# Forgetting attention: q and k of four heads in one 512-column accumulator, from two half-depth chunks

## The reference

```python
proj = x @ w_in                                    # (512, 1024) @ (1024, 4 * 1024 + 16)
q, k, v, g, f_logit = jnp.split(proj, [D, 2 * D, 3 * D, 4 * D], axis=-1)
qh, kh = _rms_norm(heads(q), qn_g), _rms_norm(heads(k), kn_g)      # 16 heads of 64
c = jnp.cumsum(jax.nn.log_sigmoid(f_logit + b_f), axis=1)
s = einsum('bhqd,bhkd->bhqk', qh, kh) * 64 ** -0.5 + (c[..., :, None] - c[..., None, :])
o = einsum('bhqk,bhkd->bhqd', softmax(where(causal, s, -1e30)), v)
h = (o * sigmoid(g)) @ w_out
```

## Time and profile before

| | us |
|---|---|
| median of 3 runs (lowest, highest) | 1371.62 (1370.80, 1373.13) |
| the profiled execution, its own time | 1372.18 |
| its span, first to last instruction | 1370.40 |
| TensorE busy | 1338.7 (98%) |
| GpSimd, ScalarE, DVE busy | 528.1, 493.6, 472.9 |
| mean granted TensorE clock | 0.995 |

### The profile page before, as it was taken

One profiled execution on the slowest core, in us unless ns is written; L12 is line 12 of the kernel. 1 busy time (PEld: TensorE's weight loads), 2 busy tenths in 40 slices (PEclk: granted clock), 3 DMA queues, 4 the chain that ended last, 5 costly groups with the idle time before them and its releaser, 6 DMA issues.

```text
span 1370.4 us, 18953 instructions
## 1 busy us (share of the span) xinstructions
PE 1338.7 (98%) x7304; PEld 1118.0 (82%) x7304; DVE 472.9 (35%) x936; ACT 493.6 (36%) x823; POOL 528.1 (39%) x421
## 2 busy tenths in 40 slices
PE   7999999799999999999999999999999999999997
PEld 6888877689888888888888888777898888888886
DVE  4364447682111111011644565544641111110105
ACT  3413266533223322211366565644232233222111
POOL 4422441215444444643234222323145444445440
PEclk9999999999999999999999999999999999999999
DMA  6301131203333332333124212212233333323321
GB/s 210 121 32 62 63 122 62 62 17 107 96 109 103 93 93 77 124 107 95 62 63 126 63 32 63 63 62 75 80 93 95 108 105 94 93 83 118 104 96 61
DMA packets 141416, 119.60 MB, mean 87 GB/s; under 512 B 5680, under 2 KB 120592, under 8 KB 141328
## 3 DMA queue, kind: packets, MB, share of 16 engines
q1 hardware_dynamic: 141088, 118.10, 27.6%
q10 hardware_dynamic: 240, 0.31, 0.1%
HBM read 116.20 MB, written 2.10 MB: 86 GB/s over the span
## 4 chain that ended last, share of the span: by engine, by line
PE 92%; DVE 4%; ACT 3%; issue 1%; DMA 0%; ACTq 0%; SPq 0%; DVEq 0%
PE banks L531 27%; PE banks L532 27%; PE banks L533 27%; PE banks L915 2%; PE banks L1073 1%; PE banks L1038 1%; PE banks L611 1%; PE banks L1054 1%; ACT w_hi L1231 1%; PE banks L933 1%; PE banks L988 1%; PE banks L975 1%; PE banks L1046 0%; DMA x_res<-in_x_dram 0%; PE banks L1024 0%
## 5 line engine op out<-in xcount | busy, mean ns | idle before, releaser
L1184 POOL TENSOR_TENSOR w_lo<-w_raw,w_hi 128x512 fp32r<-128x512 f32 x417 | 527.8, 1293 | 810.9 <-ACT w_hi L1231 657.9
L531 PE MATMUL banks<-xT_lo,w_hi 128*128 128x512 f32 (+2 forms) x1024 | 385.0, 376 | 1.3 <-DVEq L1581 1.0
L533 PE MATMUL banks<-xT_hi,w_hi 128*128 128x512 f32 (+2 forms) x1024 | 380.9, 372 | 0.0
L532 PE MATMUL banks<-xT_hi,w_lo 128*128 128x512 f32 (+2 forms) x1024 | 380.8, 372 | 0.0
L1231 ACT ACTIVATE w_hi<-w_raw 128x2048 fp32r<-128x2048 f32 (+2 forms) x106 | 198.1, 1869 | 173.4 <-PE banks L533 145.0
L531 PEld LDWEIGHTS banks<-xT_lo,w_hi 128*128 128x128 f32 (+1 forms) x1024 | 192.4, 188 | 36.3 <-issue 3.8
L533 PEld LDWEIGHTS banks<-xT_hi,w_hi 128*128 128x128 f32 (+1 forms) x1024 | 192.3, 188 | 34.0
L532 PEld LDWEIGHTS banks<-xT_hi,w_lo 128*128 128x128 f32 (+1 forms) x1024 | 192.5, 188 | 32.2
L1850 DVE TENSOR_TENSOR banks<-silu_g,banks 128x512 f32<-128x512 f32 x44 | 30.6, 696 | 402.5 <-PE banks L533 402.5
L531 PE MATMUL banks<-w_lo,xT_hi 128*128 128x256 f32 (+1 forms) x480 | 158.6, 330 | 2.5 <-issue 2.4
L533 PE MATMUL banks<-w_hi,xT_hi 128*128 128x256 f32 (+1 forms) x480 | 153.3, 319 | 0.0
(11 more groups left out here) (193 smaller groups left out, 1244.1 us busy)
## 6 DMA issues: line engine op xcount, KB each, us to landing
w_raw<-in_ffn_w_dram SPq DMA_DIRECT2D x92, 512.0 KB, 4.5
w_raw<-in_ffn_w_dram SPq DMA_DIRECT2D x20, 1024.0 KB, 4.8
w_raw<-in_fox_w_in_dram SPq DMA_DIRECT2D x16, 1024.0 KB, 5.8
w_raw<-in_even_w_in_dram SPq DMA_DIRECT2D x13, 1024.0 KB, 4.9
w_raw<-in_even_w_out_dram SPq DMA_DIRECT2D x4, 1024.0 KB, 4.8
w_raw<-in_fox_w_out_dram SPq DMA_DIRECT2D x4, 1024.0 KB, 4.8
x_res<-in_x_dram SPq DMA_DIRECT2D x4, 512.0 KB, 6.8
out_dram<-x_res SPq DMA_DIRECT2D x3, 512.0 KB, 2.6
```

The source lines that it names most:

```text
L531: mm(acc, l_hi, r_lo, start=first, stop=False)
L532: mm(acc, l_lo, r_hi, start=False, stop=False)
L533: return mm(acc, l_hi, r_hi, start=False, stop=final)
L1184: ins = nc.gpsimd.tensor_tensor(w_lo[c % RING][:, a:a + n], w_raw[c % RAW][:, a:a + n], w_hi[c % RING][:, a:a + n].bitcast(F32), ALU.subtract)
```

## The change

q and k of the same four heads come side by side in one accumulator of 512 columns. A head group (stage `foxh0` to `foxh3`) is two chunks, each of half the depth (4 of 8 row blocks) and 256 columns of q beside 256 of k, loaded by two DMAs of 512 KB. The number and size of chunks stay. A piece is now one token tile of one half: 4 x 3 = 12 matmuls of 512 columns, and a tile's accumulator is closed by its second half. Copy, square, sums, root and norm are done once for 8 heads of a tile, and the turn is four transposes into bank 3, read by two copies (one for q, one for k, since their gains differ). `sq` has one buffer and `qn` two, where they had two and three. The order of pieces is written out (`HEAD_LEAD`, `HEAD_ORDER`), and so is the list of roundings with what holds their quarters back (`fox_rounds`). `fox_start(0)` now runs four pieces, the first half and the second half of tiles 0 and 1, each first piece waiting for its own tile. The second half chunk `foxh0` is rounded in the norm before, ahead of the fourth tile's root. The quarters of both `foxh0` chunks and of the first `foxv0` chunk are waited for one by one. The copy to `c_rows` stands before the load of the second chunk of `foxh1`.

```diff
-FOX_LEAD = [("q", 0), ("k", 0), ("v", 0)]
-FOX_PARTS = [[("q", 1), ("k", 1), ("v", 2)], [("q", 2), ("k", 2), ("v", 3)], [("q", 3), ("k", 3), ("g", 0)],
-             [("g", 1), ("g", 2), ("g", 3)]]
+FOX_LEAD = [("h", 0), ("v", 0)]
+FOX_PARTS = [[("h", 1), ("v", 2)], [("h", 2), ("v", 3)], [("h", 3), ("g", 0)], [("g", 1), ("g", 2), ("g", 3)]]
+HEAD_LEAD = [(0, 0), (1, 0), (0, 1), (1, 1), (2, 0), (3, 0), (2, 1), (3, 1)]
+HEAD_ORDER = [(0, 0), (0, 1), (1, 0), (1, 1), (2, 0), (3, 0), (2, 1), (3, 1)]
...
+    def heads_major(stage, m, i, k0):
+
+        rows = m[k0 * P:(k0 + KD // 2) * P, :].rearrange("(k p) n -> p k n", p=P)
+        out.append((stage, [(256 * part, rows[:, :, part * D + 256 * i:part * D + 256 * (i + 1)], KD // 2, 256, 512)
+                            for part in range(2)], SLOT))
...
+        V0, H1, V2, H2 = (first_step(f"fox{x}") for x in ("v0", "h1", "v2", "h2"))
+        V3, H3, G0, G1 = (first_step(f"fox{x}") for x in ("v3", "h3", "g0", "g1"))
+        fox_rounds = [(V0 - 2, ("foxv0", 0), None), (V0 + 1, ("foxv0", 1), qn_of(0, 3, 3, 3, 3)),
+                      (V0 + 3, ("foxh1", 0), None), (V0 + 5, ("foxh1", 1), None),
+                      (H1 + 1, ("foxv2", 0), qn_of(1, 0, 0, 1, 1)),
+                      (H1 + 6, ("foxh2", 0), qn_of(1, 2, 2, 3, 3)), (V2 + 1, ("foxh2", 1), None),
+                      (H2 + 1, ("foxv3", 0), qn_of(2, 0, 0, 1, 1)),
+                      (H2 + 6, ("foxh3", 0), qn_of(2, 2, 2, 3, 3)), (V3 + 1, ("foxh3", 1), None),
+                      (H3 + 1, ("foxg0", 0), qn_of(3, 0, 0, 1, 1)),
+                      (H3 + 6, ("foxg1", 0), qn_of(3, 2, 2, 3, 3)), (G0 + 1, ("foxg2", 0), None),
+                      (G1 + 1, ("foxg3", 0), None), (G1 + 5, ("out1", 0), None), (G1 + 9, ("out1", 1), None)]
...
+            def heads_chunk(j, order, places=None):
+
+                stage, begun = f"foxh{j}", set()
+                for t, half in order:
+                    c, key, tok = stage_chunks[stage][half], (stage, t), slice(t * P, (t + 1) * P)
+                    if half == 0:
+                        open_bank(key, places[t] if places else next_gemm_bank(), "act")
+                    acc = psum[uses[key][0]][:, :]
...
+                    for k in range(KD // 2):
+                        if c in by_piece and c not in begun:
+                            piece_in(c, k)
+                        ins = products(acc, xT_hi[:, half * 4 + k, tok], xT_lo[:, half * 4 + k, tok],
+                                       hi(c, k * 512, 512), lo(c, k * 512, 512), half == 0 and k == 0,
+                                       half == 1 and k == KD // 2 - 1)
...
-                    wait_tiles(turned_tiles[0] + NT // 2)
-                    q0, = stage_chunks["foxq0"]
                     gemm_banks[0] = 2
-                    running["foxq0"] = token_chunk(q0, "act", xT_hi, xT_lo, 0, True, True, 256, (0, 1, 5, 6))
-                    next(running["foxq0"])
-                    next(running["foxq0"])
+                    running["foxh0"] = heads_chunk(0, HEAD_LEAD, (0, 1, 5, 6))
+                    for t in range(2):
+                        wait_tiles(turned_tiles[0] + t + 1)
+                        next(running["foxh0"])
+                    next(running["foxh0"])
+                    next(running["foxh0"])
                     return
...
-                for i in range(2):
-                    ins = nc.tensor.transpose(acc[:, i * P:(i + 1) * P], qn[:, n % 3, i * P:(i + 1) * P], ident[:, :])
+                for i in range(4):
+                    ins = nc.tensor.transpose(acc[:, i * P:(i + 1) * P], qn[:, n % 2, i * P:(i + 1) * P], ident[:, :])
...
-                if c == chunk_at("foxk1"):
+                if c == chunk_at("foxh1", 1):
                     sp.wait_ge(S["c_split"], 1)
...
                     if t == NT - 2 and tag != "n2_1":
                         hi_upto(after + 1)
+                    if t == NT - 1 and tag != "n2_1":
+                        hi_upto(after + 3)
                     ln_root(step_n, t)
...
+                for part in range(2):
+                    dst = qk[:, j % 2, part, :, t * P:(t + 1) * P]
+                    src = acc[:, 256 * part:256 * (part + 1)].rearrange("p (k n) -> p k n", k=2)
+                    ins = fn(dst, src, ACT.Copy, scale=gains[:, 4 + part:5 + part])
+                    if part == 0:
+                        step(ins)
+                release(ins, ("heads", n))
```

More of the change, by code:

```diff
@@ L369, in pieces_of @@
         def pieces_of(part):
-            return [(c, p) for name, i in part for c in stage_chunks[f"fox{name}{i}"] for p in range(PIECES)]
+            out = []
+            for name, i in part:
+                cs = stage_chunks[f"fox{name}{i}"]
+                if name == "h":
+                    out += [(cs[half], t) for t, half in (HEAD_LEAD if i == 0 else HEAD_ORDER)]
+                else:
+                    out += [(c, p) for c in cs for p in range(PIECES)]
+            return out
         F_UNITS = PAIRS * NT
@@ L390, in heads_at @@
             stage = chunks[c][0]
-            if stage[3] not in "qk":
+            if stage[3] != "h" or c != stage_chunks[stage][1]:
                 return None
-            part, j = "qk".index(stage[3]), int(stage[4])
-            return part, j, p, (2 * j + part) * NT + p
+            j = int(stage[4])
+            return j, p, j * NT + p
         def values_at(i):
@@ L412, in build, with first_step, qn_of @@
         TURN_LAG = 4
[L413 to L428, removed]
+        def first_step(stage, n=0):
+            return [i for i, (piece, _) in enumerate(fox_steps) if piece and piece[0] == stage_chunks[stage][n]][0]
+        def qn_of(j, *tiles):
+            return [("qn_done", j * NT + t + 1) for t in tiles]
+        V0, H1, V2, H2 = (first_step(f"fox{x}") for x in ("v0", "h1", "v2", "h2"))
[9 more added lines that the diff above has]
+                      (G1 + 1, ("foxg3", 0), None), (G1 + 5, ("out1", 0), None), (G1 + 9, ("out1", 1), None)]
+        round_at, lo_behind = {}, {}
+        for i, (stage, n), behind in fox_rounds:
+            round_at[i] = stage_chunks[stage][n]
+            if behind:
+                lo_behind[stage_chunks[stage][n]] = behind
         lo_behind[stage_chunks["out0"][2]] = [("oe_lo", AH)] * 4
@@ L559, in token_chunk @@
                 nk = size // width
-                if stage == "foxq0":
+                if c in by_piece:
                     pe.wait_ge(hi_ready, c + 1)
@@ L570, in token_chunk @@
                     for k in range(nk):
[L571 to L575, removed]
+                        if c in by_piece and t == 0:
+                            piece_in(c, k)
                         tok = slice(t * P, (t + 1) * P)
@@ L584, in token_chunk, with piece_in @@
                         if final:
+                            used_with_bank(c, key)
+                        else:
+                            used_alone(c, ins)
+                    yield
+            def piece_in(c, k):
+                if k < PIECES - 1:
+                    pe.wait_ge(S["fox_lo"], (PIECES - 1) * by_piece.index(c) + k + 1)
+                else:
+                    pe.wait_ge(lo_ready, c + 1)
+            def heads_chunk(j, order, places=None):
[5 more added lines that the diff above has]
+                    acc = psum[uses[key][0]][:, :]
+                    if c not in begun:
+                        if c in by_piece:
+                            pe.wait_ge(hi_ready, c + 1)
+                        else:
+                            weights_in(c)
+                    for k in range(KD // 2):
+                        if c in by_piece and c not in begun:
+                            piece_in(c, k)
+                        ins = products(acc, xT_hi[:, half * 4 + k, tok], xT_lo[:, half * 4 + k, tok],
+                                       hi(c, k * 512, 512), lo(c, k * 512, 512), half == 0 and k == 0,
+                                       half == 1 and k == KD // 2 - 1)
+                    begun.add(c)
+                    if half == 1:
+                        close_bank(key, ins)
+                    if t == NT - 1:
+                        if half == 1:
                             used_with_bank(c, key)
@@ L1078, in _ @@
             for i, (piece, s) in enumerate(fox_steps):
-                if piece and i >= 2:
+                if piece and i >= 4:
                     stage = chunks[piece[0]][0]
                     if stage not in running:
-                        if stage == "foxk0":
-                            running[stage] = token_chunk(piece[0], "act", xT_hi, xT_lo, 0, True, True, 256, (7, 2, 0, 1))
+                        if stage[3] == "h":
+                            running[stage] = heads_chunk(int(stage[4]), HEAD_ORDER)
                         elif stage == "foxv0":
@@ L1117, in load @@
                     sp.wait_ge(lo_ready, c - RAW + 1)
-                for off, src, a, b in chunks[c][1][which]:
```

(6 more changed lines are left out.)

61 lines of the change are left out of this document (31 added, 30 removed).

## The result

The changed kernel takes 1376.03 us (median of 7 runs, 1374.40 to 1377.01) where the kernel before takes 1371.62: ratio 1.0029, interval 1.0018 to 1.0041. Repeated beside more runs, the ratio was 1.0019 (1.0009 to 1.0028). So it is slower by 0.2 to 0.3%, some 3 to 4 us, where I had forecast 0.0.

What follows compares the result with a forecast made beforehand. TensorE was taken to bound the kernel (98% busy, 92% of the chain). Terms -3.5 + 5.8 + 2.7 + 1.5 + 0.5 - 4.0 - 3.0 = 0.0 us left the median at 1371.6 us, range 1367.0 to 1376.5.

Steps and rivals of the forecast that it cites:

- Part 1: Projections of q and k: 32 pieces of 12 matmuls of 512 columns, 0.11 us less each, -3.5 us.
- Part 2: Opening: TensorE waits 4.1 us for the second half chunk, then 1.7 us for its later quarters, +5.8 us.
- Part 3: First chunk of v: TensorE waits 1.0 us for its late rounding, then 1.7 us for quarters, +2.7 us.
- Part 6: Opening: TensorE's clock falls to half behind the 4.1 us wait, +0.5 us.
- rival (d): Clock stays down past the first half chunks, through the start of the forget projection: +5.1 us, 1376.7 us; chance 0.07.
- Part 5: Old waits go: -4.0 us in the opening, -3.0 of 3.2 us in the parts, waits for ScalarE's copies.
- Part 4: Second chunk of heads 4 to 7, needed sooner, its load issued late: +1.5 us, bounds 0 and 3.
- rival (c): ScalarE keeps TensorE waiting in the parts as before, and brings part 4's chunk late: +4.5 us, 1376.1 us; chance 0.18.

Runs made afterwards that it cites:

- quarter free: The changed kernel with the fourth low quarter of the first half chunk of heads not held for the third norm: ratio 1.0004 to the kernel before.
- three edits: Changed kernel, first half chunk's fourth quarter not held, v's first chunk rounded one step earlier, gates' copy behind one more load: ratio 0.9972 to the kernel before.
- both with the wait filled: Changed kernel, forget projection's first half in TensorE's long wait: 1.0035 to the kernel before; with the fourth tile's root ahead of the early rounding too: 1.0036.
- the kernel before with the quarter free: The kernel before, with the fourth low quarter of its first q chunk not held for the third norm: ratio 1.0018 to the kernel before.
- the fastest kernel: Changed kernel, first half chunk's fourth quarter not held, both v roundings one step earlier, gates' copy behind one more load: 1363.16 us, 0.9934 to the kernel before.
- both moves and the copy: Changed kernel with both of v's chunks rounded one step earlier and the gates' copy behind one more load: ratio 0.9963 to the kernel before.

## Why the prediction was wrong

Most terms held. **Part 1**: 3 to 3.5 us; two pieces of 12 between two units take 5.65 to 5.70 us. The formula that part 1 quotes from the Trainium skill (TensorE: Matmul & The Clock Gate, section Back-to-back issue gap) is not the only figure there: the section calls it the gap of an isolated matmul, and for a stream of weight loads and matmuls has about 131 ns at 512 columns. An unbroken row of them took 227 ns each here. **Part 2**: a wait of 4.05 us from start to start, 3.8 beyond the usual 0.23, where I had 4.1; and the 24 matmuls behind it took 7.3 us to the fourth tile's turn where 24 of 0.23 take 5.5, so 1.9 us for quarters and half clock, where I had 1.7 + 0.5. **Part 3**: 3.3 us where I had 2.7. **Part 6** as said, and the clock was back before the turn, so rival (d) is out: the window shows 3.3 us of it.
```profile
680.50:683.80 3.30, 3.30 (x9) 1.99 (x8) 3.23 (x3) 0.00 (x0) 2.97 (x3) 0.50 0.03 5
```
**The step that failed** is the end of the opening, in the account from part 3 to part 5. I stopped at the first chunk of v, took v's second chunk for ready, and wrote all the copies' waits off as gone. Its rounding is instead the last of a row on ScalarE (a root that waits for DVE, a gate operation) and came late: 0.8 us at the turn, and 1.5 at the piece (it started 1.83 us behind the turn, where 0.35 is usual), 2.3 us that I had put at nothing. Moving that rounding removed both.

**Part 4** had the right mechanism and the wrong size: 2.3 us where I took 1.5 (inside its bounds). I placed the load's issue at 722.3, 2 to 4 us later than before; on the clock of the profile before (this stage began 1.5 us later) it came at 725.3, 5.8 later. The gates were 2.3 us behind already, the rounding of v's second chunk now lies between the two table-bound gate operations (1.92 us, where a copy of 0.47 lay), and the six DVE operations on the gates take 6.2 us in place of 4.0, beside GpSimd's split of that chunk. The load landed 5.9 us later, as priced; TensorE came for it 2.4 us later than I had it, for the most part by the late v. Moving the copy removed the whole.

**Part 5** in the parts: of the 3.2 us, 2.3 went where I took 3.0. A wait of 1.14 us from start to start at 754.28, 0.9 beyond the usual, is new and stands in every variant of the changed kernel. It is for the copy to `q_raw`, which ScalarE makes behind a unit's exponentials and a copy of turned probabilities:
```profile
752.39 0.58 ACT L1605 ACTIVATE p_fox<-banks,small 128x384 f32<-128x384 f32 x1
...
753.18 0.28 ACT L1533 ACTIVATE pT_fox<-banks 128x128 f32<-128x128 f32 x1
753.63 0.60 ACT L1316 ACTIVATE q_raw<-banks 128x512 f32<-128x512 f32 x1 [0.18 <-ACT pT_fox L1533]
```
This is a small piece of rival (c), not the rival.

The account, measured less forecast. In the opening: parts 2 and 6 -0.6 (5.7 us for 6.3), part 3 +0.6, v's second chunk +2.3, products and turns -0.4 (by difference). In the parts: part 4 +0.8, the rest +0.5 (by difference). Together 3.2 us, against the 3.1 of the stage. That the first two cancel is luck. The prices of part 3, of v's second chunk and of part 4 are shown by removal; the wait at 754.28 was not removed. The two ratios put the changed kernel 2.6 to 4.0 us above, around the 3.1. In the table, a stage with the wait ahead of it and the ratio agree within about 1 us for every kernel; what makes up that last microsecond, with one profile of each, stays open.

The measured time is the 1376.1 us of rival (c), but not by its mechanism: ScalarE was late in the opening, at v, and hardly in the parts. I had looked for it where the products are made, not where the list of roundings changed.

The Trainium skill (GPSIMD Engine Reference, section 1. Specifications) has GpSimd's SBUF interfaces shared with VectorE, with contention for DVE instructions that have two SBUF inputs. The traces agree: 1.28 us became 2.42 for the norm's operation and 0.17 became 1.20 for the tiny ones, while the reduction from `sq`, of one input, took its 0.69 us beside GpSimd as well. The operation on `c_parts` at 720.31 has one input too and took 1.32 us instead of 0.42; the page counts a two-port mode among the slowed ones, and no row says whether this one runs in it.

## What to carry to other kernels

When work is brought forward or its operands are needed sooner, walk the whole row of roundings and loads behind it, not only the first: each late chunk here was a position in a list or a hold, and four small edits of these turned +3 us into -9. A hold that protects one engine should be priced again after each change of order, on both sides: here it was worth 1.4 us before and cost 2.9 after. And before a wait is filled with other work, ask what that work covers where it stands.

## What the runs showed of the hardware

The clock fell to half for 3.3 to 3.5 us, and not only behind the wait of 4 us. In the two kernels with one chunk of v moved it fell behind the wait of 2.3 us, which in the changed kernel, at the same size, it did not. In four (quarter free, three edits, both with the wait filled) it fell behind the wait of 1.2 us at v's second chunk, which in the changed kernel it did not either. In the kernel before with the quarter free it fell at 671 us, near no wait above 1.4 us. In the fastest kernel it stayed full in the whole stage. Each fall cost about 1.6 us beside work that was ready (eight matmuls at 0.43 instead of 0.23 us). So a wait removed can be followed by a fall at the next one, and single edits show less than they are worth: the two moves of v showed 1.4 and 0.8 us alone, and without their falls 3.0 and 2.4; with the copy's 2.9 these add up to the stage that both moves and the copy showed together, 311.6 us. What decides whether it falls, these runs don't settle. The Trainium skill (TensorE: Matmul & The Clock Gate, section HAM oscillation) tells of waits in mid-kernel that bring the low clock back; these traces agree that they can, and show the clock falling behind a wait of one size in some kernels and not in others.

The smallest DVE operations suffer most beside GpSimd's subtraction by the factor: 7, against 1.9 for the norm's operation on 1024 elements a partition. In microseconds they lose about the same, 1.03 and 1.14. The rows suggest why. In the changed kernel GpSimd makes four quarters from 705.77 in 4.99 us, so they end near 709.5 and 710.8 (an estimate, by equal spacing; TensorE's matmuls that wait for them start at 709.57 and 710.81), and the two slow operations of 8 elements end at 709.54 and 710.77. For the second half chunk, four quarters from 678.50 in 4.96 us end near 679.7, 681.0 and 682.2, and three slow operations of one element end there as well:
```profile
679.09 0.69 DVE L1866 SCALAR_TENSOR_TENSOR stats<-stats 128x1 f32<-128x1 f32 x1 [4.71 <-ACT stats L1312]
679.82 1.20 DVE L1867 SCALAR_TENSOR_TENSOR stats<-stats 128x1 f32<-128x1 f32 x1
681.05 1.20 DVE L1868 SCALAR_TENSOR_TENSOR stats<-stats 128x1 f32<-128x1 f32 x1
```
So it looks as if each were held until the quarter in progress was done, and a chain of tiny operations loses about a quarter's time at each link. That is read from these rows; no run here varied the length of a quarter.
